# Output gates projected last and channel by channel, their product taken in PSUM by VectorE

## What is computed

```python
p = modulate(x, shift, scale) @ w_in        # 3072 columns: q, k, v, g, a, b of 512 each
q, k = rope(q), rope(k) / 8                 # 8 heads of 64
o = retention_forward(q, k, v) + retention_backward(q, k, v)
ret = silu(g) * (group_norm(o) * gn_w + gn_b)           # per head of 64
u = depthwise_conv31(a * sigmoid(b)) + conv_b
conv = silu(layer_norm(u) * cln_w + cln_b)
mix = concatenate([ret, conv]) @ w_out      # 1024 x 1024
x = layer_norm(alpha * x + gate1 * mix)
x = layer_norm(alpha * x + gate2 * (relu(modulate(x) @ w1)**2 @ w2))
```

## Time and profile before

| what | us |
|---|---|
| median of 3 runs (2905.45 to 2911.14) | 2907.34 |
| the profiled execution, its own time | 2907.55 |
| its span, first to last instruction | 2905.7 |
| mean granted clock of TensorE, share of 2.4 GHz | 0.97 |

### The profile page before, as it was taken

One profiled execution on the slowest core, in us unless ns is written; L12 is line 12 of the kernel. 1 busy time (PEld: TensorE's weight loads), 2 busy tenths in 40 slices (PEclk: granted clock), 3 DMA queues, 4 the chain that ended last, 5 costly groups with the idle time before them and its releaser, 6 DMA issues.

```text
span 2905.7 us, 38116 instructions
## 1 busy us (share of the span) xinstructions
PE 2726.5 (94%) x13644; PEld 2242.3 (77%) x13644; DVE 1966.5 (68%) x3283; ACT 719.2 (25%) x1490; POOL 1083.0 (37%) x1081
## 2 busy tenths in 40 slices
PE   6999999797999999999999699998888999999996
PEld 4778878576888888888888478888677888888885
DVE  4699983856776677677668889873765454454456
ACT  3233334534111111111111323334433111111111
POOL 1344454754111111111112645564762323323325
PEclk9999999798999999999999899999899999999998
DMA  8322322621222222222220222212521111111111
GB/s 244 94 85 76 101 75 82 181 76 45 66 72 70 81 72 72 72 72 73 73 38 29 83 66 61 62 50 58 159 73 44 51 43 51 51 43 51 51 43 66
DMA packets 246658, 214.69 MB, mean 74 GB/s; under 512 B 60384, under 2 KB 203280, under 8 KB 246544
## 3 DMA queue, kind: packets, MB, share of 16 engines
q1 hardware_dynamic: 149488, 120.94, 13.9%
q10 hardware_dynamic: 97056, 92.29, 10.4%
HBM read 190.56 MB, written 22.63 MB: 73 GB/s over the span
## 4 chain that ended last, share of the span: by engine, by line
PE 82%; DVE 8%; POOL 4%; DMA 2%; issue 1%; ACT 1%; SPq 1%; POOLq 0%; ACTq 0%; DVEq 0%
PE bank L624 15%; PE bank L626 15%; PE bank L625 15%; PE bank L1146 9%; PE bank L1147 9%; PE bank L1148 9%; PE bank L708 1%; PE bank L1008 1%; PE bank L1079 1%; PE bank L1009 1%; PE bank L1010 1%; PE bank L1053 1%; DVE x_hl L1620 1%; PE bank L1078 1%; PE bank L1064 1%
## 5 line engine op out<-in xcount | busy, mean ns | idle before, releaser
L1583 POOL TENSOR_TENSOR w_lo<-raw,w_hi 128x1024 fp32r<-128x1024 f32 x120 | 288.4, 2404 | 1124.8 <-ACT w_hi L1414 1124.8
L1850 DVE TENSOR_TENSOR work<-work 128x512 f32<-128x512 f32 (+1 forms) x160 | 158.0, 987 | 472.1 <-ACT work L1402 471.2
L1146 PE MATMUL bank<-x_hl,w_hi 128*128 128x512 f32 (+1 forms) x1280 | 475.4, 371 | 0.0
L1147 PE MATMUL bank<-x_hl,w_hi 128*128 128x512 f32 (+1 forms) x1280 | 473.2, 370 | 0.0
L1148 PE MATMUL bank<-x_hl,w_lo 128*128 128x512 f32 (+1 forms) x1280 | 472.9, 369 | 0.0
L1874 DVE TENSOR_TENSOR work<-work,bank 128x512 f32<-128x512 f32 x576 | 390.1, 686 | 122.3 <-PE bank L626 111.4
L624 PE MATMUL bank<-w_hi,h_hi 128*128 128x512 f32 x1152 | 451.1, 392 | 7.3 <-DVE work L1874 5.4
L625 PE MATMUL bank<-w_lo,h_hi 128*128 128x512 f32 x1152 | 449.5, 390 | 0.0
L626 PE MATMUL bank<-w_hi,h_lo 128*128 128x512 f32 x1152 | 449.3, 390 | 0.0
L1755 DVE SCALAR_TENSOR_TENSOR bank<-work,bank 128x512 f32<-128x512 f32 (+1 forms) x580 | 406.9, 702 | 17.8
L1414 ACT ACTIVATE w_hi<-raw 128x1024 fp32r<-128x1024 f32 x120 | 126.8, 1059 | 775.6 <-PE bank L626 583.9
(11 more groups left out here) (141 smaller groups left out, 4575.1 us busy)
## 6 DMA issues: line engine op xcount, KB each, us to landing
raw<-in_w_ff ACTq DMA_DIRECT2D x128, 512.0 KB
work<-in_w_ada SPq DMA_DIRECT2D x48, 512.0 KB
plain_words<-in_w_ada ACTq DMA_DIRECT2D x64, 256.0 KB
raw<-in_w_in SPq DMA_DIRECT2D x60, 256.0 KB
plain_words<-in_w_ada SPq DMA_DIRECT2D x16, 512.0 KB, 12.6
raw<-in_w_out SPq DMA_DIRECT2D x10, 512.0 KB
gate_rows<-work SPq DMA_DIRECT2D x72, 64.0 KB, 1.6
retention_rows<-work SPq DMA_DIRECT2D x72, 64.0 KB, 1.6
```

What stands on the lines that cost most here:

```text
L1146: nc.tensor.matmul(o, slot(mlp_slot(l, f), 0)[:, wc], x_hi[:, k, cols], start=k == 0, stop=False)
L1147: nc.tensor.matmul(o, slot(mlp_slot(l, f), 0)[:, wc], x_lo[:, k, cols], start=False, stop=False)
L1583: nc.gpsimd.tensor_tensor(slot(mlp_slot(l, sl), 1), raw[:, un % 2, :], slot(mlp_slot(l, sl), 0).bitcast(F32), ALU.subtract).then_inc(w_rea ...
L1850: nc.vector.tensor_tensor(a32, a32, a32, ALU.mult).then_inc(S["h_sq"], 1)
```

## The change

- **Groups.** Q steps of all four pairs make q, k and v only (384 columns); there are no K and G halves. A new last group G makes the gates of all heads channel-major, like AB: per run of tokens and 128 channels one F step (runs of 256 tokens, 24 matmuls of 256) or a G and an H step (runs of 512 tokens, 12 matmuls of 512 each, in one bank). It adds four units, the 256 words of g per unit leave the Q units (768 words are split instead of 1024).
- **Gates.** ScalarE takes silu in the evacuation of F and H steps (128x512) and SP stores the result to `gate_columns`. Later the tile's gates are loaded as four blocks of 128 channels.
- **Retention half.** After the transposes ScalarE applies the group norm's weight and bias per channel in PSUM (four operations of 128x128), VectorE multiplies by the gates in PSUM, ScalarE writes the high part (`ret_high`), VectorE the low part. GpSimd's three operations and the two loads of rows (gn_w, gn_b) go.
- **Early tiles.** For the first three tiles (EARLY) the loads, the norms, the transposes and the splits are entries of the plan, placed under the gate steps. The loop behind the plan starts at tile 3; TensorE runs `turn_mix(j+1)`, `turn_conv(j+3)`, `project_mix(j)`.
- **Order and banks.** A turn before a Q step gets 6 x 256 of `room`, not 7 x 256. Scores and values keep one bank each to the end. Output products go to banks 2 and 6, transposed tiles to 3 and 7. SP's loop issues `cv_load(j)`, `o_load(j)`, `gate_load(j)`, `residual(j-2)`.

```diff
-GROUPS = [("AB", 0), ("AB", 1), ("Q", 0), ("AB", 2), ("Q", 1), ("AB", 3), ("Q", 2), ("Q", 3)]
-IN_HALVES = (3,)
+GROUPS = [("AB", 0), ("AB", 1), ("Q", 0), ("AB", 2), ("Q", 1), ("AB", 3), ("Q", 2), ("Q", 3), ("G", 0)]
+EARLY = 3
+QKV = 3 * P
...
+        elif kind == "G":
+            for r, (_, nt) in enumerate(chunks_of(layer)):
+                steps += [(part, c, r) for c in range(PAIRS) for part in ("GH" if nt == 4 else "F")]
...
+            if not posts:
+                hoisted += [(n + 1, ("cv_load", 0)), (n + 1, ("cv_load", 1))]
+                for j in range(EARLY):
+                    hoisted += [(n + 3 + 2 * j, ("cvt", j)), (n + 4 + 2 * j, ("cnorm", j))]
...
-            room = 7 * 2 * P // (1 if kind == "Q" and t in tiles else 2) if kind in "QKG" else 3 * P * chunks_of(layer)[t][1]
+            room = 6 * 2 * P // (1 if t in tiles else 2) if kind == "Q" else 3 * P * chunks_of(layer)[t][1]
...
+            gated = max(i for i, st in enumerate(steps) if st[0] in "FH" and st[2] == run)
+            turn = max(n + 7, gated + 3, turn + 2)
+            hoisted += [(n, ("o_load", j)), (max(n, gated + 1), ("g_load", j)), (n + 3, ("gn_cent", j)), (n + 4, ("gn_var", j)),
+                        (n + 5, ("gn_scale", j)), (turn, ("mixtr", j)), (turn + 1, ("mixlo", j))]
...
+                def gate_load(j):
...
+                    for par in range(2):
+                        sp.wait_ge(S["g_st"][par], s0["g_st"] + 16 * PAIRS // 2 * (run + 1))
+                    if j >= 2:
+                        sp.wait_ge(S["ret_y"], s0["ret_y"] + j - 1)
+                    gates_of(j)
...
-                for j in range(2, n):
-                    sp.wait_ge(S["cvt_done"], s0["cvt_done"] + j - 1)
-                    o_rows_of(j)
-                    cv_rows_of(j)
...
-                    sp.wait_ge(S["mix_a"], s0["mix_a"] + j - 1)
-                    gates_of(j)
-                    residual(j - 2)
+                sp.wait_ge(S["comb_done"], s0["comb_done"] + n * PAIRS)
+                for j in range(EARLY, n):
+                    cv_load(j)
+                    o_load(j)
...
+                    gate_load(j)
+                    for i in range(0 if j == EARLY else j - 2, j - 1):
+                        residual(i)
...
+                for j in range(n):
+                    if EARLY <= j + 1 < n:
+                        turn_mix(j + 1)
+                    if EARLY <= j + 3 < n:
+                        turn_conv(j + 3)
+                    project_mix(j)
...
+                def mix_high(j):
...
+                    for k in range(4):
+                        turned = ps_m[0][:, k * P:(k + 1) * P]
+                        last = nc.scalar.activation(turned, turned, ACT.Identity,
+                                                    bias=gnc[:, 1, k:k + 1], scale=gnc[:, 0, k:k + 1])
+                    last.then_inc(S["ret_aff"], 1)
...
+                        elif kind in "FH":
+                            g, w = counted["gate"][i], chunks_of(l)[t][1] * P
...
+                            nc.scalar.activation(g_out[:, g % 2, 0:w], ps[:, 0:w], ACT.Silu).then_inc(S["gate_done"], 1)
...
-                        nc.gpsimd.tensor_tensor(o, o, rows[:, 0, :], ALU.mult).then_inc(S["gn_aff"], 1)
...
-                        nc.gpsimd.tensor_tensor(o, o, rows[:, 1, :], ALU.add).then_inc(S["gn_aff"], 1)
...
-                        nc.gpsimd.tensor_tensor(o, o, g_in[:, j % 2, :], ALU.mult).then_inc(S["mix_a"], 1)
...
+                def low_part(j):
+
+                    turned = ps_m[0][:, :].rearrange("p (a b) -> p a b", b=P)
+                    dve.wait_ge(S["ret_aff"], s0["ret_aff"] + j + 1)
+                    dve.wait_ge(S["g_in"][j % 2], s0["g_in"] + 16 * (j // 2 + 1))
+                    nc.vector.tensor_tensor(turned, turned, g_in[:, j % 2, :, :], ALU.mult).then_inc(S["ret_y"], 1)
+                    dve.wait_ge(S["mix_hi"], s0["mix_hi"] + j + 1)
...
+                    dve.wait_ge(S["ret_hi"], s0["ret_hi"] + j + 1)
+                    nc.vector.tensor_tensor(x_lo[:, 0:4, cols], turned, x_hi[:, 0:4, cols].bitcast(F32), ALU.subtract).then_inc(S["ret_lo"], 1)
...
+                for st in range(EARLY, n + 4):
                     if st >= 4:
                         combine(st - 4)
                     if st < n:
                         centre(st)
+                        conv_stats(st)
+                    if EARLY <= st - 1 < n:
+                        conv_shift(st - 1)
                         scale_heads(st - 1)
+                    if EARLY <= st - 2 < n:
                         low_part(st - 2)
                     if st < n:
                         variance(st)
```

More of the change, by code:

```diff
@@ L146, in mix_in_plan @@
     group_end = {last_step(UNIT_OF[g] + (1 if g[0] == "AB" else 3)) for g in GROUPS}
[L147 removed]
+    plan, evacs, posts, ready = [], list(range(len(steps))), [i for i, st in enumerate(steps) if st[0] == "Q"], []
     scored, valued, evac_at, taps = set(), set(), {}, []
[L149 removed]
+    posted, scans = set(), [[(p, k) for p in range(PAIRS) for k in range(1, NT)] for _ in range(2)]
     items = [(p, t) for p in range(PAIRS) for t in item_order(layer, p)]
@@ L153, in mix_in_plan @@
     finished, stored, pause, consumed, fetches = [], [], 3, False, [5]
+    hoisted, waiting, turn = [], list(range(EARLY)), 0
     def load_units(count):
@@ L202, in mix_in_plan @@
             kind, p, t = steps[evacs[0]]
-            if kind in "QK" and p and t in tiles and (p - 1, t) not in valued:
+            if kind == "G":
+                evacs.pop(0)
+                continue
+            if kind == "Q" and p and t in tiles and (p - 1, t) not in valued:
                 break
@@ L225, in mix_in_plan @@
                 p, j = scans[d][0]
-                if (p, order[j - 1]) not in keyed or p and order[j] in tiles and (p - 1, order[j]) not in valued:
+                if (p, order[j - 1]) not in posted or p and order[j] in tiles and (p - 1, order[j]) not in valued:
                     break
@@ L229, in mix_in_plan @@
                 scans[d].pop(0)
-        while items and items[0] in asked and items[0] in keyed:
+        while items and items[0] in posted:
             p, t = items[0]
@@ L263, in mix_in_plan @@
             plan.append(("masks",))
+        while waiting and (PAIRS - 1, tiles[waiting[0]]) in valued:
+            j = waiting.pop(0)
+            run = next(r for r, (t0, nt) in enumerate(chunks_of(layer)) if t0 <= tiles[j] < t0 + nt)
+            gated = max(i for i, st in enumerate(steps) if st[0] in "FH" and st[2] == run)
+            turn = max(n + 7, gated + 3, turn + 2)
+            hoisted += [(n, ("o_load", j)), (max(n, gated + 1), ("g_load", j)), (n + 3, ("gn_cent", j)), (n + 4, ("gn_var", j)),
+                        (n + 5, ("gn_scale", j)), (turn, ("mixtr", j)), (turn + 1, ("mixlo", j))]
+        hoisted.sort(key=lambda x: x[0])
+        plan += [entry for due, entry in hoisted if due <= n]
+        hoisted = [x for x in hoisted if x[0] > n]
         n += 1
@@ L277, in step_counts @@
         "A": before(lambda kind, i, t: kind == "A"),
-        "rope": before(lambda kind, i, t: kind in "QKG"),
-        "kv": before(lambda kind, i, t: kind in "QK"),
-        "gate": before(lambda kind, i, t: kind == "G" or kind == "Q" and t in tiles),
-        "turned": before(lambda kind, i, t: kind in "QKG" and t in tiles)}
+        "Q": before(lambda kind, i, t: kind == "Q"),
+        "gate": before(lambda kind, i, t: kind in "FH"),
+        "turned": before(lambda kind, i, t: kind == "Q" and t in tiles),
+        "bank": [sum(st[0] != "G" for st in steps[:i]) % PROJ_BANKS for i in range(len(steps))]}
 def shape_constants():
@@ L1699, in _ @@
                         before, at = (F_ORDER, B_ORDER)[d][k - 1:k + 1]
-                        posted = min(counted["kv"][i] for i, st in enumerate(steps) if st[0] in "QK" and st[1:] == (p, before))
-                        dve.wait_ge(S["u_evac"], s0["u_evac"] + posted + 1)
+                        dve.wait_ge(S["u_evac"], s0["u_evac"] + counted["Q"][steps.index(("Q", p, before))] + 1)
                         if p and at in T:
@@ L1808, in _ @@
-                centre(0)
-                variance(0)
-                scale_heads(0)
-                for st in range(1, n + 4):
+                for st in range(EARLY, n + 4):
                     if st >= 4:
```

613 lines of the change are left out of this document (312 added, 301 removed).

## The result

The changed kernel takes 2929.49 us (median of four runs, 2927.35 to 2931.99), the kernel before 2909.07 in the same session (2905.45 to 2911.14): a ratio of 1.0076, 95% interval 1.0061 to 1.0090. It is slower by 20 us; 2897 had been forecast, with 2916 as the upper end, which the measured time passes by 13.5.

The account below looks back on a forecast made before the run. TensorE and VectorE were taken to bound the long projection stretch together, with seams waiting on loads and chains. Gains of 3.5 us in layer 0 and 7 in layer 1 took 2907.55 to 2897 us, range 2875 to 2916.

Parts of the forecast that it names:

- the early tiles' normalisation beside the gates: Normalisation of the first three tiles, placed under the gate steps, was to lie hidden there and cost nothing.
- the output loop: First half of the output projection: 75 us in layer 0 against 72.8 before, 56.4 in layer 1 against 57.2.
- the stretch up to Q2: Projections up to the end of group Q2: gains 29 and 19 us, ending at 373 and 1916 us.
- the seam: Gates' end to first output projection: 6.6 us for a load plus 1.4 at half clock, bounds 4 and 9.
- the fast loop: Rival, output loop: loads land sooner, so it runs at VectorE's 7.3 us a tile; 2886 us, chance 0.20.
- Projections: Projection steps: 384-column matmuls follow each other after 0.173 us; total even, each Q step of pairs 0 to 2 loses 1.3 us.
- VectorE alone ends Q2 at 401.7 - 23.6: Layer 0 up to Q2: VectorE sets the end, 30 fewer taps saving 23.6 us, some 8 more if waits vanish.
- Q3 and the gates: From Q2's end to the gates' end: 149 us in layer 0, bounds 518 to 528 for the end; 119 in layer 1.
- 2 to 4 us if late: Gates' weights waiting for their slots until the last Q3 tile: costed at nothing, 2 to 4 us if late.
- the ring: Output loop: a tile's loads queue on SP behind the wait for an earlier tile's ret_y; 9.3 us per tile.
- VectorE holds TensorE in the Q steps: Slower rival: VectorE's 6.9 us delays TensorE's 6.1 us Q steps; 2945 us, or 2921 if half lost; chance 0.18.
- Nothing: Rival: the seam's idle only moves elsewhere, or the three early tiles are unready when gates end; 2906 us, chance 0.20.

Follow-up runs that it names:

- e4_both: Changed kernel with SyncE's loop loads issued ahead of the wait for ret_y and ScalarE's early-tile operations one plan step later; 2880.62 us, ratio to before 0.9912.
- e6: Against e4_both, fewer VectorE taps in the plan step that holds seven scans, the taps following in later steps; 2870.79 us.
- e3: Against the changed kernel, normalisation, transposes and gating of the three early tiles begin only after the last retention item; 2917.94 us.
- e2: Against the changed kernel, ScalarE's operations for early tiles issued one plan step later, behind the next retention item's diagonal copies; 2903.81 us.
- e5: Against e4_both, ScalarE's split of the output projection's first weight block one to two plan steps later, the two behind it shifted too; 2873.83 us.
- e7: Against e4_both, convolution-column and retention-row loads of tiles 3 and 4 issued five steps before the gates end; 2874.89 us.
- e1: Against the changed kernel, SyncE issues a tile's convolution columns and retention rows ahead of the previous tile's gates; 2902.81 us.

## Why the prediction was wrong

**The direction failed in two terms of the sum: the early tiles' normalisation beside the gates, put at nothing, and the output loop, put at 75 and 56.4 us.** They cost 39 and 17 us more than forecast. That the miss is 32 and not 56 is luck: the stretch up to Q2 and the seam came out 25 us better, for reasons that the forecast did not have. With two orders of issue mended (e4_both) the kernel takes 2880.6 us, below even the 2886 of the fast loop, so that the change itself is sound.

*Projections.* Right. A 384-column matmul follows the last after 0.17 us, as taken:
```profile
313.83 0.33 PE L652 MATMUL bank<-h_hi,x_hl 128*128 128x384 f32 x1
314.00 0.33 PE L650 MATMUL bank<-h_hi,x_hl 128*128 128x384 f32 x1
```
*The stretch up to Q2.* Better than forecast, by 6.6 and 13.8 us. The step that failed is "VectorE alone ends Q2 at 401.7 - 23.6": TensorE is busy for 309.2 of 316.8 us, and 202.1 of 204.5 in layer 1, and while a Q group runs it hardly idles at all. Q1 and Q2 of layer 0 (columns as in the earlier trace rows):
```profile
211.80:270.60 58.80, 58.80 (x365) 53.77 (x363) 55.50 (x115) 21.04 (x71) 34.23 (x66) 1.00 0.22 67
307.90:366.40 58.50, 58.18 (x359) 53.60 (x355) 55.35 (x114) 20.26 (x68) 31.99 (x65) 1.00 0.23 73
```
So TensorE sets the end, and VectorE, busy for 278 and 195 us, has room. The 363 and 1904 that TensorE alone was to give were nearly met. Before, too, TensorE was busy for 347 of 351 us and VectorE for 307, so it was not "as full as TensorE": VectorE's busy share is 0.88 in both kernels. It had looked like a second bound since it hardly waited for another engine, but its taps are rationed by TensorE's steps. The ration's count was near: 33 taps of 512 fewer by the end of Q2 in layer 0 (229 before, 196 after), 30 worked out.

*Q3 and the gates.* Q3 took 73.3 and 61.4 us. Of the forecast's 149 and 119 that leaves 76 and 58 for the gates, which took 97 and 75. (The forecast didn't divide the two; some 6 us of the excess belong to Q3's step behind the scans, e6.) The sentence that failed is "the three tiles' normalisation lie[s] under the gates", costed at nothing. Its work does fit: ScalarE is busy for 40 of 97 us. What I did not ask is what stands behind the waiting square: the copies for the next item, and so TensorE. An item's 1.34 us was not the fault. Before, items already stood beside half steps of 2.88 us, and a turn took 4.3 us:
```profile
489.43 0.36 PE L624 MATMUL bank<-w_hi,x_hl 128*128 128x256 f32 x1
...
493.73 0.36 PE L624 MATMUL bank<-w_hi,x_hl 128*128 128x256 f32 x1
```
In e3, beside gate steps of 2.73 us and without early tiles, a turn takes 4.0 to 4.1 us, which is 2.73 and 1.34. It is the early tile's work put ahead of the item's on ScalarE that makes it 6.3. e2 gives 24 us of it back in the two layers. Next, "2 to 4 us if late" was allowed for the gates' own weights; the block that was late is the first of the output projection, it held ScalarE and not TensorE's weights, and cost 5.6 us (e5).

*The seam.* Right in its mechanism and within its bounds, 3 and 2 us shorter than 6.6 + 1.4 (the 1.3 and 4.8 named there make 6.1): 5.0 and 6.0 us, ended by the load of convolution columns behind the last gate store. In layer 0 this load is issued 1.1 us after the gates' end, and TensorE's wait for it ends 3.1 us behind the issue; e7 takes 4.5 us off each layer by moving the load.

*The output loop.* The mechanism was right, the size was off in two terms, and that failed the forecast here. "The issues of gates and residual on SP 0.85": VectorE's centre needs the rows of o, the fourth issue and not the third, and from the multiply's end (576.18) to that issue (577.75) it is 1.6 us. The landing is 4.8 behind it, as taken, and from centre to the multiply's end it is 3.9 us where 3.65 were taken, so the ring is 10.3, not 9.3. And "tiles 0 to 2 need no transposes and run 6 us each" forgot that TensorE's order puts transposes of tiles 3 to 6 ahead of the projections of tiles 0 to 3, and with them the waits for their loads: the first three periods are 10.9, 9.2 and 10.5 us. With the landing of 3.0 us that only the gates' load had, the ring would still have been 8.5, an estimate (10.3 - 4.8 + 3.0).
The Trainium skill's price for a DMA (DMA: Bandwidth & Descriptors, "Anatomy of one DMA"), stated for GpSimd's path, gives an estimate of 2.6 us for these 256 KB. It does not fit the loads that end the ring, issued by SyncE: their medians are 4.8 and 5.0 us in the changed kernel and 4.4 and 4.8 with the order of e1.

*The rivals.* "VectorE holds TensorE in the Q steps" had the right sign and the wrong place. In layer 0 it occurs mainly in two steps behind a burst of scans, not in each, and did not decide. "Nothing" named "the three early tiles are not ready when the gates end"; they were ready, and what delayed the gates was the making ready. What should have been a rival: an early tile's operation holds the item queued behind it.

## What to carry to other kernels

Work that is hoisted into another stage must be placed on each engine's queue, not only under its busy share: for each operation that waits for another engine, look up what stands behind it and how soon a third engine needs that. Where two chains of dependent work share the in-order queues of several engines, a price read for one chain alone (here 1.34 us an item) holds only if no operation of the other waits ahead of it. Where a loop's load is issued behind a wait for the same loop's result, count every issue up to the one that the consumer needs, or issue loads a tile ahead.

## What the runs showed of the hardware that I had not expected

Short waits of TensorE cost more than themselves: what it does next can run at the lower of its two clocks (1.2 GHz, granted clock 0.50). In the gates of layer 0 the same 432 matmuls and small products keep it busy for 83.8 us at a mean granted clock of 0.91 and for 77.8 at 0.96 when most of the waits are gone (e4_both); in the output loop 72.2 us at 0.91 and 65.5 at 0.98. That is 6 to 7 us in each, beside the idle time itself. In the kernel before the long seam stood at half clock (0.50) and the output loop at 0.98; in the changed one the seam is at 0.90, and waits of 1 to 5 us stand inside the gates and the loop.
